# One step of a hybrid encoder layer on one core: where relu and square of the MLP's Strassen part run, and when mix's rows are stored

## The chip, the cores and the metric

The kernel runs on one core of one Trainium2 chip. The metric is the device time of one launch in microseconds (us). Three runs of the kernel before gave 2861.73, 2862.52 and 2863.64 us; the median is 2862.52 us.

The engines by the profile's names: PE is TensorE (matmuls) and PEld its weight loads, DVE is VectorE, ACT is ScalarE, POOL is GpSimd, SP is SyncE, which here only issues DMAs. PEq, ACTq and so on are the engines' instruction queues.

## The reference, cut to what matters

One layer works on 2048 prompt rows and 64 sample rows of width 1024, all in float32:

```python
h = rms_norm(x, g_pre_mix)
q, k, v, logf, gate_b, cu = project(h, w_in, b_f)
merged = concat(rms_norm(attention(q, k, v, logf)), rms_norm(gate_b * short_conv(cu)))
x = x + rms_norm(merged @ w_o, g_post_mix)          # "mix"
h2 = rms_norm(x, g_pre_mlp)
m = square(relu(h2 @ w_up)) @ w_down                # w_up 1024x4096, w_down 4096x1024
x = x + rms_norm(m, g_post_mlp)
```

Outputs are x for both row sets, the new keys, values, forget logs and the last rows of the convolution.

## The kernel before, in words

Float32 products are made of three matmuls on rounded operands: a value is split into a rounded high part (`hi`, type fp32r, usually written by ACT with a Copy) and the rest (`lo`, written by POOL or DVE as value minus hi), and hi*hi + hi*lo + lo*hi is summed in PSUM.

Three stages follow one another: input projection with attention, the output projection "mix" (`mix_rows`), and the MLP (`mlp`). All order is written out by hand: each engine has its own program, and semaphores join them (`wait_ge`, `then_inc`). An engine runs its program strictly in order, so an instruction that waits holds up all behind it on that engine.

**Mix.** The loop goes over 17 row tiles (tile 0 is the 64 sample rows) in software-pipelined steps t. In step t ACT squares the inputs of tile t+1 (L1782), rounds its convolution half (L1786), squares tile t-1's mixed rows (L1800), takes a root (L1804), squares the new x (L1808, with the store of x2, L1810), takes the next root (L1812), copies the attention part (`take_part`, L1819) and copies the transposed h2 of tile t-1 out of PSUM (`back_out`, L1827). `store_h2` issues the store of h2 to HBM on ACT's queue. For the first five tiles ("split", stored in hi and lo) it stands in front of `back_out` and stores tile t-2; for all later ones it stands behind `back_out` and stores tile t-1, the tile just copied (L1833). `h2_hi` has two slots, so `back_out` of tile t-1 waits until the store of tile t-3 has landed. PE transposes h2 (L2020) between the products of one tile and the next; it needs h2 from DVE (L1923), which stands at the end of the chain L1800, L1804, DVE's scaling and adding, L1808, L1812.

**MLP.** The rows are in three groups. Group 0 (5 tiles) is computed plainly. Groups 1 and 2 (6 row tiles each) make their first layer by Strassen's scheme: the hidden axis has 16 chunks of 256 columns, and for each chunk `up` makes 7 products of 12 matmuls (128x384) instead of 8. `down` then multiplies the 256 hidden values into 6 row tiles, 12 matmuls (128x512) each, in two alternating PSUM buffers. PE's order is up(chunk n+1), down(chunk n), up(n+2), and so on.

For a chunk, ACT copies the first product to SBUF (`take`, L2575); DVE's `combine` adds the other products (`plus`, L2683) into four results c11, c12, c21, c22 in the buffers `stage`, and applies relu and square to each in one instruction in place (`square`, L2669). Between them it makes four weight sums for the chunk after (`make_sum`, L2666), which the 7 products need. ACT's `hidden_first` waits until PE has done 3 (first half: c11, c12) or all 6 tiles (second half: c22, c21) of the previous `down`, since the hidden buffer is single, and copies them rounded (L2586); POOL's `hidden_rest` makes the lo part (L2454). After `combine` DVE adds each finished tile of `down` into y (`add`, L2728; L2726 in a group's first chunk). PE's third tile waits for the first add, the fourth for the second, and so on.

PE waits for DVE in three more places of `up`: products 5, 6 and 7 reuse PSUM buffers, and wait for `take`, the first `plus` and the c11 `plus`. The last stands behind the first weight sum, which waits for the DMA of the next raw weights.

At a group's end the finished rows are normalised: ACT squares and sums (`deviation`, L2597, and L2599), DVE scales (`scale`, L2771), POOL adds x (`out_rows`, L2462), SP stores (`store_y`). Four deviations stand on ACT between the two halves of `hidden_first`, and the remaining ones follow `take` of the next chunk. On SP the load of the raw weights of the chunk after next is queued behind the store of the group's second row tile, which waits for POOL's second `out_rows`. The late scales of a group stand in the next `combine` on DVE.

Of the kernel before, what the change touches and what calls it, by code (L numbers as in the profile page):

```python
# [7 lines left out]
ALU = mybir.AluOpType  # L8
ACT = mybir.ActivationFunctionType
# [20 lines left out]
RT = QT + 1  # L30
# [1618 lines left out]
def mix_rows(nc, io, dr, sem, ident, early, front, block, last_rows):  # L1649
# [8 lines left out]
    with ctx:  # L1658
# [25 lines left out]
        def at(t):  # L1684

            if isinstance(t, int) and t == 0:
                return SEQ, DEC
            return (t - 1) * P, P

        def run(eng, step):  # L1690

            for t in range(7):
                step(t, t % 2)
            with eng.Fori(0, 2) as i:
                step(2 * i + 7, 1)
                step(2 * i + 8, 0)
            for t in range(11, RT + 1):
                step(t, t % 2)

        def is_split(t):  # L1700

            return isinstance(t, int) and t < FIRST_TILES
# [7 lines left out]
        def is_tile(t):  # L1710
            return not isinstance(t, int) or 0 <= t < RT
# [65 lines left out]
        def _(act):  # L1777
# [51 lines left out]
            def store_h2(t, s):  # L1829
                row, n = at(t)  # L1830
                if not is_split(t):
                    act.wait_ge(S["h2_hi_done"], 2 * t + 2)
                    act.dma_start(dr["h2_t"].rearrange("(k p) r -> p k r", p=P)[:, :, bass.ds(row, n)], h2_hi[:, s, :, 0:n].bitcast(F32)).then_inc(h2_stored[s], 16)  # L1833
                    return
                act.wait_ge(S["h2_lo_done"], 2 * t + 2)
                for part, name in ((h2_hi, "h2_hi"), (h2_lo, "h2_lo")):
                    act.dma_start(dr[name].rearrange("(k p) r -> p k r", p=P)[:, :, bass.ds(row, n)], part[:, s, :, 0:n].bitcast(F32)).then_inc(h2_stored[s], 16)
# [5 lines left out]
            def step(t, s):  # L1843
                last, nxt = not isinstance(t, int) or t >= 1, is_tile(t + 1)
                if nxt:
                    front_squares(t + 1, 1 - s)
                final = isinstance(t, int) and t == RT
                if final:
                    act.wait_ge(S["c_mult"], RT)
                    early.split_first(act, 0)  # L1850
                if last:
                    back_squares(t - 1)
                    back_root(t - 1)
                if final:
                    early.split_first(act, 1)
                if nxt:
                    front_turned(t + 1, 1 - s)
                    if not last:
                        take_part(t, s)
                    front_root(t + 1, 1 - s)  # L1860
                if last:
                    back_second(t - 1, 1 - s)
                if is_tile(t) and last:
                    take_part(t, s)
                if is_split(t - 2) and t >= 2:
                    store_h2(t - 2, s)
                if last:
                    back_out(t - 1, 1 - s)
                    if not is_split(t - 1):
                        store_h2(t - 1, 1 - s)  # L1870

            run(act, step)

        @block.vector
        def _(dve):
# [223 lines left out]
def mlp(nc, io, dr, sem, early, front):  # L2099
# [13 lines left out]
    with ctx:  # L2113
# [19 lines left out]
        stage = [tile("m_stage0", [P, 3 * P])]  # L2133
# [45 lines left out]
        c11_taken, c12_taken, c21_taken, c22_taken = sem("m_c11_taken"), sem("m_c12_taken"), sem("m_c21_taken"), sem("m_c22_taken")  # L2179
        u_done = sem("m_u_done")  # L2180
# [12 lines left out]
        def chunk(g, i):  # L2193

            return CHUNKS * (g - 1) + i
# [56 lines left out]
        def is_first(g, i):  # L2252
            return isinstance(i, int) and i == 0
# [256 lines left out]
        def _(act):  # L2510
# [65 lines left out]

            def hidden_first(g, i, which):
                n, w = chunk(g, i), GROUP_COLS[g]
                if is_first(g, i):
                    act.wait_ge(dn_done, tiles_before(g, i) - (0 if which or g == 1 else COUNT[g - 1] - 3))  # L2580
                else:
                    act.wait_ge(dn_done, tiles_before(g, i - 1) + (COUNT[g] if which else 3))
                for r, b, src, seen in ((0, 0, 0, 1), (0, 1, 2, 3)) if which == 0 else ((1, 1, 3, 2), (1, 0, 1, 4)):
                    act.wait_ge(u_done, 4 * n + seen)
                    for x, hi, _ in hidden_parts(g, b, r, stage[src][:, 0:w]):
                        first = act.activation(hi, x, ACT.Copy)  # L2586
                    first.then_inc(u_hi_done, 1)
# [65 lines left out]
        def _(dve):  # L2653
# [11 lines left out]
                                (t1[:, :, :], b22, ALU.subtract, t2[:, :, :]), (t4[:, :, :], b21, ALU.subtract, t2[:, :, :]))[r]  # L2665
                dve.tensor_tensor(to, x, z, op).then_inc(sums_made, 1)  # L2666

            def square(x):
                return dve.scalar_tensor_tensor(x, x, 0.0, x, ALU.max, ALU.mult)  # L2669

            def combine(g, i, late=(), ahead=None):

                def sums(r):
                    if ahead:
                        make_sum(*ahead, r)

                n, w = chunk(g, i), GROUP_COLS[g]
                bank = [up_bank[b][:, 0:w] for b in BANK_OF]
                c11, c21, c12, c22 = (x[:, 0:w] for x in stage)

                def plus(j, to, x, done):
                    dve.wait_ge(multiplied, PRODUCTS * n + j + 1)
                    dve.tensor_tensor(to, bank[j], x, ALU.add).then_inc(done, 1)  # L2683

                later = not isinstance(n, int) or n >= 1
                dve.wait_ge(p1_taken, n + 1)
                if later:
                    dve.wait_ge(u_lo_done, 4 * n - 2)
                plus(1, c12, c11, p6_added)
                sums(0)  # L2690
                plus(2, c11, c11, c11_taken)
                dve.wait_ge(c11_taken, n + 1)
                square(c11).then_inc(u_done, 1)
                sums(1)
                dve.wait_ge(p6_added, n + 1)
                if later:
                    dve.wait_ge(u_lo_done, 4 * n)
                plus(3, c21, c12, p7_added)
                sums(2)
                dve.wait_ge(p7_added, n + 1)  # L2700
                plus(4, c22, c21, c22_taken)
                plus(4, c12, c12, p5_added)
                dve.wait_ge(c22_taken, n + 1)
                square(c22).then_inc(u_done, 1)
                sums(3)
                for f in late[:1]:
                    scale(f)
                dve.wait_ge(p5_added, n + 1)
                plus(5, c12, c12, c12_taken)
                dve.wait_ge(c12_taken, n + 1)  # L2710
                square(c12).then_inc(u_done, 1)
                plus(6, c21, c21, c21_taken)
                dve.wait_ge(c21_taken, n + 1)
                square(c21).then_inc(u_done, 1)
                for f in late[1:]:
                    scale(f)

# [281 lines left out]
```

## Time and profile before

| | |
|---|---|
| median of 3 runs | 2862.52 us |
| profiled execution, its own time | 2863.82 us |
| its span | 2862.2 us |
| PE busy | 2700.8 us, 94% |
| DVE busy | 1743.7 us, 61% |
| POOL busy | 1322.6 us, 46% |
| ACT busy | 998.1 us, 35% |
| mean granted TensorE clock | 0.987 of full speed |

A group of instructions is shown as line, engine, operation, output<-input, sizes, count, then busy time and mean time of one. The span counts from the first to the last instruction of the profiled execution; its own time is 1.6 us more. "Idle before" is the time an engine did nothing ahead of an instruction, with the instruction that released it. Times on a timeline are us from the span's start. Mix's loop lies at about 1107 to 1340, group 0 of the MLP at 1340 to 1804, group 1 from 1784, group 2 from about 2300.

### The profile page before, as it was taken

How to read it: one execution, taken by the hardware profiler on the slowest of the kernel's cores; microseconds unless marked ns; L12 is line 12 of the kernel's file. 1: busy time of each engine (PE TensorE's matmuls, PEld its weight loads, DVE VectorE, ACT ScalarE, POOL GpSimd, SP SyncE). 2: the span in 40 equal slices, each digit the busy share in tenths (PEclk: the TensorE clock that was granted, in tenths of full speed). 3: DMA queues.
4: the chain of work that ended last, by engine and by line, in shares of the span. 5: the costliest groups of instructions: out<-in, count | busy, mean ns of one | idle time of the engine just before them, and what ended most of it. 6: DMA issues, size and time to landing. Idle time of an engine off the chain costs nothing.

```text
span 2862.2 us, 42917 instructions
## 1 busy us (share of the span) xinstructions
PE 2700.8 (94%) x14966; PEld 2415.6 (84%) x14966; DVE 1743.7 (61%) x2744; ACT 998.1 (35%) x1831; POOL 1322.6 (46%) x883
## 2 busy tenths in 40 slices
PE   8999999999999999998999998899999989999997
PEld 8899899998787787877888887788888878888886
DVE  5333443348787886665445555777667756667775
ACT  3201201117787776544232322322222232222222
POOL 4233334311100126452567675765566657556664
PEclk9999999999999999999999999999999999999999
DMA  6534535665433443675344446422112352211213
GB/s 196 188 114 125 159 102 153 208 177 126 120 95 97 110 143 89 204 205 162 115 169 158 161 150 240 145 71 72 59 59 73 119 212 88 73 59 59 73 59 103
DMA packets 294358, 364.21 MB, mean 127 GB/s; under 512 B 37577, under 2 KB 245393, under 8 KB 290129
## 3 DMA queue, kind: packets, MB, share of 16 engines
q1 hardware_dynamic: 257152, 316.15, 36.1%
q0 software_dynamic: 11808, 26.74, 2.9%
q10 hardware_dynamic: 25264, 19.66, 2.0%
q8 instruction: 69, 1.13, 0.2%
q14 instruction: 65, 0.52, 0.1%
HBM read 264.30 MB, written 97.94 MB: 127 GB/s over the span
## 4 chain that ended last, share of the span: by engine, by line
PE 20%; DVE 13%; issue 10%; POOL 6%; DMA 2%; SPq 0%; ACT 0%; DVEq 0%; POOLq 0%; ACTq 0%
PE dn_bank L2902 13%; PE up_bank L2877 6%; DVE m_t L2666 4%; DVE m_raw_up L2666 3%; DVE m_stage L2683 3%; POOL m_pieces L2438 2%; POOL m_up_plain L2415 2%; DMA m_raw_up<-in_w_up 2%; POOL m_u L2431 2%; DVE m_y L2728 1%; PE up_bank L2833 1%; PE dn_bank L2857 1%; DMA m_raw_dn<-in_w_down 1%; DVE m_y L2771 1%; DVE m_stage L2669 1%
## 5 line engine op out<-in xcount | busy, mean ns | idle before, releaser
L2902 PE MATMUL dn_bank<-m_w_dn,m_u 128*128 128x512 f32 x2304 | 543.0, 394 | 39.6 <-DVE m_y L2728 29.2
L2902 PEld LDWEIGHTS dn_bank<-m_w_dn,m_u 128*128 128x128 f32 x2304 | 434.0, 190 | 140.9 <-DVE m_y L2728 38.7
L2877 PE MATMUL up_bank<-m_h,m_w_up 128*128 128x384 f32 x2688 | 476.3, 337 | 10.3 <-DVE m_stage L2683 6.5
L2877 PEld LDWEIGHTS up_bank<-m_h,m_w_up 128*128 128x128 f32 x2688 | 470.8, 189 | 14.0 <-issue 11.4
L2728 DVE TENSOR_TENSOR m_y<-dn_bank,m_y 128x1024 f32<-128x1024 f32 x180 | 217.6, 1220 | 194.4 <-PE dn_bank L2902 194.1
L508 POOL TENSOR_TENSOR w_lo<-w_raw,w_hi 128x1024 fp32r<-128x1024 f32 x72 | 181.0, 2518 | 327.8 <-DVE w_hi L722 327.8
L2454 POOL TENSOR_TENSOR m_u<-m_stage,m_u 128x384 fp32r<-128x384 f32 x128 | 130.5, 1040 | 280.7 <-ACT m_u L2586 280.7
L2411 POOL TENSOR_TENSOR m_w_up<-m_raw_up,m_w_up 128x512 fp32r<-128x512 f32 x128 | 196.2, 1552 | 83.0 <-ACT m_w_up L2560 83.0
L2743 DVE TENSOR_TENSOR m_u<-m_u 128x320 f32<-128x320 f32 (+1 forms) x64 | 109.3, 1747 | 174.9 <-ACT m_u L2540 174.9
L2586 ACT ACTIVATE m_u<-m_stage 128x384 fp32r<-128x384 f32 x128 | 60.1, 517 | 438.6 <-PE dn_bank L2902 437.5
L938 PE MATMUL proj<-ha_hi,w_hi 128*128 128x384 f32 (+1 forms) x640 | 212.2, 332 | 0.0
L1452 DVE TENSOR_TENSOR p_lo<-t_bank,p_hi 128x512 fp32r<-128x512 f32 (+1 forms) x336 | 198.4, 600 | 20.3 <-ACT p_hi L1393 18.0
L2833 PEld LDWEIGHTS up_bank<-m_h,m_up_plain 128*128 128x128 f32 x1536 | 206.4, 189 | 4.6 <-issue 2.0
L938 PE MATMUL proj<-ha_hi,w_lo 128*128 128x384 f32 (+1 forms) x640 | 210.1, 328 | 0.0
L938 PE MATMUL proj<-ha_lo,w_hi 128*128 128x384 f32 (+1 forms) x640 | 210.0, 328 | 0.0
L2833 PE MATMUL up_bank<-m_h,m_up_plain 128*128 128x256 f32 (+1 forms) x1536 | 208.0, 295 | 1.7 <-PEq L2966 1.7
L1349 POOL TENSOR_TENSOR att<-o_n 128x256 f32<-128x256 f32 (+1 forms) x40 | 26.2, 656 | 392.2 <-ACT o_n L1404 387.9
L1393 ACT ACTIVATE p_hi<-t_bank 128x512 fp32r<-128x512 f32 (+1 forms) x336 | 171.8, 528 | 71.3 <-PE t_bank L1490 67.2
L2683 DVE TENSOR_TENSOR m_stage<-up_bank,m_stage 128x384 f32<-128x384 f32 x224 | 119.9, 546 | 93.9 <-PE up_bank L2877 93.9
L2560 ACT ACTIVATE m_w_up<-m_raw_up 128x512 fp32r<-128x512 f32 x128 | 76.4, 625 | 251.0 <-PE up_bank L2877 221.6
L2447 POOL TENSOR_TENSOR m_w_dn<-m_raw_dn,m_w_dn 128x2048 fp32r<-128x2048 f32 x32 | 147.8, 4620 | 20.4 <-ACT m_w_dn L2568 20.2
L2411 POOL TENSOR_TENSOR m_w_up<-m_t,m_w_up 128x512 fp32r<-128x512 f32 x96 | 151.7, 1607 | 0.0
(290 smaller groups left out, 5809.5 us busy)
## 6 DMA issues: line engine op xcount, KB each, us to landing
m_raw_up<-in_w_up SPq DMA_DIRECT2D x48, 1024.0 KB, 5.4
m_raw_dn<-in_w_down SPq DMA_DIRECT2D x48, 1024.0 KB, 4.9
w_raw<-in_w_in SPq DMA_DIRECT2D x72, 512.0 KB, 4.1
scratch_h_pairs<-m_pieces POOLq DMA_DIRECT2D x12, 1792.0 KB, 7.8
m_h<-scratch_h_pairs SPq DMA_DIRECT2D x14, 1536.0 KB, 11.2
nck<-scratch_ncum SPq DMA_DIRECT2D x8, 1312.0 KB, 18.6
scratch_v_hl<-vhl SPq DMA_DIRECT2D x20, 512.0 KB, 2.7
q_hi<-scratch_q_hi SPq DMA_DIRECT2D x16, 528.0 KB, 6.9
```

The source lines that it names most:

```text
L508: pool.tensor_tensor(w_lo[:, slot(i)], w_raw[:, i % 2], w_hi[:, slot(i)].bitcast(F32), ALU.subtract).then_inc(w_lo_done, 1)
L938: mm = pe.matmul(out[:, 0:CW[g]], w[:, slot(i), k], h[g][:, k, chunk(g, n)], start=(k == 0 and a == 0), stop=(k == KB - 1 and a == 2))
L1393: act.activation(p_hi[:, x.p, x.cols], t_bank[x.at % T_BANKS][:, x.cols], ACT.Copy).then_inc(hi_done, 1)
L1452: dve.tensor_tensor(p_lo[:, x.p, x.cols], t_bank[x.at % T_BANKS][:, x.cols], p_hi[:, x.p, x.cols].bitcast(F32), ALU.subtract).then_inc(lo_ ...
L2411: pool.tensor_tensor(w_up[:, j, 1], sources[j], w_up[:, j, 0].bitcast(F32), ALU.subtract).then_inc(w_lo_done, 1)
L2447: pool.tensor_tensor(w[:, 1], raw[:, :, :], w[:, 0].bitcast(F32), ALU.subtract).then_inc(dn_lo_done, 1)
L2666: dve.tensor_tensor(to, x, z, op).then_inc(sums_made, 1)
L2683: dve.tensor_tensor(to, bank[j], x, ALU.add).then_inc(done, 1)
L2728: dve.tensor_tensor(place, bank[:, :], place, ALU.add).then_inc(y_added, 1)
L2833: mm = pe.matmul(up_bank[2 * x + b][:, 0:w], up_first[:, cc, wp, k, b * P:(b + 1) * P], early.rows[2 * x + hp][:, k, :], start=(k == 0 and ...
L2877: mm = pe.matmul(out, w_up[:, j, wp, k, :], hidden_rows(g, j, hp, k), start=(k == 0 and p == 0), stop=(k == KH - 1 and p == 2))
L2902: mm = pe.matmul(bank[:, cols], part, wd[:, wp, b, cols], start=(b == 0 and p == 0), stop=(b == 1 and p == len(passes) - 1))
```

## The change

The MLP: DVE's `square` and its waits go. ACT's `hidden_first` gets, for each of the two results of its half, a wait for the result, a Relu in place and a Square in place (the Square waits for the Relu), and then one wait for both, all ahead of the wait for PE's tiles. The rounding copies stay as they are. Mix: the store of h2 is ahead of `back_out` for every tile, and stores tile t-2; the last tile's store follows the loop.

```diff
             def step(t, s):
...
-                if is_split(t - 2) and t >= 2:
+                if not isinstance(t, int) or t >= 2:
                     store_h2(t - 2, s)
                 if last:
                     back_out(t - 1, 1 - s)
-                    if not is_split(t - 1):
-                        store_h2(t - 1, 1 - s)
 
             run(act, step)
+            store_h2(RT - 1, (RT - 1) % 2)
...
             def hidden_first(g, i, which):
                 n, w = chunk(g, i), GROUP_COLS[g]
+                for m, (src, taken) in enumerate(((0, c11_taken), (2, c12_taken)) if which == 0 else ((3, c22_taken), (1, c21_taken))):
+                    x = stage[src][:, 0:w]
+                    act.wait_ge(taken, n + 1)
+                    act.activation(x, x, ACT.Relu).then_inc(u_done, 1)
+                    act.wait_ge(u_done, 8 * n + 4 * which + 2 * m + 1)
+                    act.activation(x, x, ACT.Square).then_inc(u_done, 1)
+                act.wait_ge(u_done, 8 * n + 4 * which + 4)
                 if is_first(g, i):
                     act.wait_ge(dn_done, ...)
                 else:
                     act.wait_ge(dn_done, ...)
-                for r, b, src, seen in ((0, 0, 0, 1), (0, 1, 2, 3)) if which == 0 else ((1, 1, 3, 2), (1, 0, 1, 4)):
-                    act.wait_ge(u_done, 4 * n + seen)
+                for r, b, src in ((0, 0, 0), (0, 1, 2)) if which == 0 else ((1, 1, 3), (1, 0, 1)):
                     for x, hi, _ in hidden_parts(g, b, r, stage[src][:, 0:w]):
                         first = act.activation(hi, x, ACT.Copy)
...
-            def square(x):
-                return dve.scalar_tensor_tensor(x, x, 0.0, x, ALU.max, ALU.mult)
...
                 plus(2, c11, c11, c11_taken)
-                dve.wait_ge(c11_taken, n + 1)
-                square(c11).then_inc(u_done, 1)
                 sums(1)
...
                 plus(4, c12, c12, p5_added)
-                dve.wait_ge(c22_taken, n + 1)
-                square(c22).then_inc(u_done, 1)
                 sums(3)
...
                 plus(5, c12, c12, c12_taken)
-                dve.wait_ge(c12_taken, n + 1)
-                square(c12).then_inc(u_done, 1)
                 plus(6, c21, c21, c21_taken)
-                dve.wait_ge(c21_taken, n + 1)
-                square(c21).then_inc(u_done, 1)
```

## Rows read from the trace of the kernel before

**Rows 1.** The page, part 1: busy time, share of the span and instructions.

```profile
PE 2700.8 (94%) x14966; PEld 2415.6 (84%) x14966; DVE 1743.7 (61%) x2744; ACT 998.1 (35%) x1831; POOL 1322.6 (46%) x883
```

**Rows 2.** Timeline of PE in the Strassen groups: start, length, instructions, idle before.

```profile
1902.43 11.18 PE L2902 MATMUL dn_bank<-m_w_dn,m_u 128*128 128x512 f32 x48 [0.93 <-DVE m_y L2728]
...
1998.96 11.17 PE L2902 MATMUL dn_bank<-m_w_dn,m_u 128*128 128x512 f32 x48 [0.94 <-DVE m_y L2728]
2009.98 14.74 PE L2877 MATMUL up_bank<-m_h,m_w_up 128*128 128x384 f32 x84
...
2788.16 11.20 PE L2902 MATMUL dn_bank<-m_w_dn,m_u 128*128 128x512 f32 x48 [0.94 <-DVE m_y L2728]
```

**Rows 3.** Timeline of DVE, a middle chunk's end and the last chunk's last product.

```profile
2028.30 0.54 DVE L2683 TENSOR_TENSOR m_stage<-up_bank,m_stage 128x384 f32<-128x384 f32 x1
2029.87 1.21 DVE L2728 TENSOR_TENSOR m_y<-dn_bank,m_y 128x1024 f32<-128x1024 f32 x1
...
2813.97 0.56 DVE L2683 TENSOR_TENSOR m_stage<-up_bank,m_stage 128x384 f32<-128x384 f32 x1 [0.86 <-PE up_bank L2877]
```

**Rows 4.** DVE's squares, all 128: duration in ns, minimum, median, maximum.

```profile
L2669 DVE SCALAR_TENSOR_TENSOR m_stage<-m_stage x128: 540/1069/2386, 1794.2 to 2814.6; 128x384 f32<-128x384 f32 x128
```

**Rows 5.** Timeline of ACT in the same middle chunk.

```profile
2002.09 0.94 ACT L2586 ACTIVATE m_u<-m_stage 128x384 fp32r<-128x384 f32 x2 [6.72 <-PE dn_bank L2902]
2010.25 0.94 ACT L2586 ACTIVATE m_u<-m_stage 128x384 fp32r<-128x384 f32 x2 [7.22 <-PE dn_bank L2902]
```

**Rows 6.** Timelines of PE, ACT, POOL and DVE where group 1 begins.

```profile
1816.12 6.82 PE L2877 MATMUL up_bank<-m_h,m_w_up 128*128 128x384 f32 x24 [3.81 <-ACT m_stage L2575]
1827.25 3.38 PE L2877 MATMUL up_bank<-m_h,m_w_up 128*128 128x384 f32 x12 [4.31 <-DVE m_stage L2683]
...
1839.29 11.18 PE L2902 MATMUL dn_bank<-m_w_dn,m_u 128*128 128x512 f32 x48 [2.70 <-DVE m_y L2726]
...
1807.39 1.06 ACT L2597 ACTIVATE m_junk<-m_y 64x1024 bf16<-64x1024 f32 x1 [2.45 <-DVE m_y L2763]
...
1814.00 2.35 POOL L2462 TENSOR_TENSOR m_y<-m_y,m_x 128x1024 f32<-128x1024 f32 x1 [1.16 <-DVE m_y L2771]
...
1824.06 2.58 DVE L2666 TENSOR_TENSOR m_raw_up<-m_raw_up 128x512 f32<-128x512 f32 x1 [6.17 <-DMA m_raw_up<-in_w_up]
```

**Rows 7.** The same where group 2 begins: PE, DVE and POOL.

```profile
2312.61 2.34 PE L2877 MATMUL up_bank<-m_h,m_w_up 128*128 128x384 f32 x12 [0.38 <-DVE m_stage L2683]
...
2324.65 13.66 PE L2902 MATMUL dn_bank<-m_w_dn,m_u 128*128 128x512 f32 x48 [4.25 <-DVE m_y L2728]
...
2352.60 2.31 PE L2877 MATMUL up_bank<-m_h,m_w_up 128*128 128x384 f32 x12 [1.78 <-DVE m_stage L2683]
...
2368.13 14.07 PE L2902 MATMUL dn_bank<-m_w_dn,m_u 128*128 128x512 f32 x48 [7.74 <-DVE m_y L2726]
...
2311.30 0.69 DVE L2666 TENSOR_TENSOR m_raw_up<-m_raw_up 128x512 f32<-128x512 f32 x1 [6.70 <-DMA m_raw_up<-in_w_up]
...
2323.39 2.34 DVE L2728 TENSOR_TENSOR m_y<-dn_bank,m_y 128x1024 f32<-128x1024 f32 x2
...
2358.61 2.38 DVE L2669 SCALAR_TENSOR_TENSOR m_stage<-m_stage 128x384 f32<-128x384 f32 x1
...
2358.18 2.39 POOL L2462 TENSOR_TENSOR m_y<-m_y,m_x 128x1024 f32<-128x1024 f32 x1 [6.75 <-DVE m_y L2771]
```

**Rows 8.** Mix: timelines of ACT and PE; landing of the x2 stores (L1810).

```profile
1236.35 1.09 ACT L1827 ACTIVATE h_hi<-h_bank 128x512 f32<-128x512 f32 x2 [1.34 <-PE h_bank L2020]
1237.60 0.38 ACTq L1833 DMA_DIRECT2D scratch_h_t<-h_hi  x1
1238.08 0.63 ACT L1782 ACTIVATE junk_a<-a_in 128x512 f32<-128x512 f32 x1 [0.64 <-ACT h_hi L1827]
...
1209.22 1.09 PE L2020 MATMUL h_bank<-ident,h 128*128 128x128 f32 x8 [1.25 <-DVE h L1923]
...
1288.93 1.10 PE L2020 MATMUL h_bank<-ident,h 128*128 128x128 f32 x8 [0.96 <-DVE h L1923]
...
DMA to landing us min/median/max: 2.6/5.5/11.7
```

## The prediction, made before the run

> **What bounds the kernel now.** I read the page's busy times first: PE is busy for 94% of the span, no other engine for more than 61% [rows 1]. So PE sets the time, and a change that leaves the matmuls alone can only give back PE's idle time or slow spells. There are about 160 us outside PE's busy time; the question is how many of these the change touches. The second view was the timeline of PE, of which I kept the rows with idle time before them. In the Strassen groups the same row comes back every 32.18 us: 48 matmuls of `down` (the third to sixth tile) start after 0.94 us of idle, released by DVE's add [rows 2]. I count 25 such rows: 13 in group 1 (first 1902.43, last 2288.55) and 12 in group 2 (2434.16 to 2788.16). Around them lie the larger stalls at the two group changes [rows 6, 7], and in mix seven short ones before the transposes [rows 8]. Third, the timelines of DVE, ACT and POOL for what ended each of these.
>
> **Steady chunks.** Take the chunk whose `up` starts at 2009.98. `up` takes 14.74 us for 84 matmuls, less a small overlap: `down` follows 14.58 later. Had DVE been free, the last `plus` could have started when the seventh product came, 14.77 us after the start: in the last chunk, where DVE makes no weight sums, that is 2813.97 against 2799.20 for PE [rows 3]. In the middle chunk it starts at 2028.30, so 18.32, and the first add at 2029.87, so 19.89; yet the first tile of `down` is done about 17.5 us after the start (14.58 plus one sixth of the 16.8 us that six tiles take). DVE is late by 2.35 us there; PE, having a second buffer, loses 0.94 of it.
>
> The change takes four squares of mostly 1.07 us from DVE ahead of this add, starts overlapping by some 0.08: 4.0 us. A square can take as little as 0.54 [rows 4], and the difference might be waiting for POOL that passes to the next instruction; then only 4 x 0.54 = 2.16 us go. Both exceed 0.94, and with DVE no earlier than the seventh product (14.77 + 0.56 = 15.3) it then waits for the first tile. The whole 0.94 goes, the period becomes 31.24 us. What is late next: nothing on DVE; PE has its next `up` buffers freed by `plus` instructions that all come earlier.
>
> On ACT each chunk gains 8 instructions. None of this shape is there with Relu, but a rounding copy from the same buffer is: two in 0.94 us [rows 5]. Lower bound 0.47 each, upper bound, with the wait of Square for Relu, 0.60; I take 0.55, so 2.2 us per half. What hides it: ACT sits idle for 6.72 us before the first half's copies and 7.22 us before the second half's [rows 5], each time for PE's tiles. Queued behind the new waits on ACT are the copies, `take` and the weight copies. c12's `plus` ends about 15.3 us after the start, just as ACT is through with its last weight copy (2027.5, or 17.5, before, and pulled forward by the earlier sums), so the four instructions end near 18 and the copies are due at 22. POOL's lo parts and PE's wait for them do not move. If the cover were gone, each us would fall on the copies, then on `take`, which product 5 needs only 8.4 us into `up`: still some 5 us of slack. Cost on the path: nothing.
>
> The stall at 2288.55 I leave to the group change below: 24 x 0.94 = **22.6 us**.
>
> **First group change [rows 6].** PE loses 3.81 + 4.31 + 2.70 = 10.8 us. (a) The 3.81 is `take` on ACT, which stands behind four deviations and the second half's copies. The deviations wait 2.45 us for DVE's fold, which follows `combine` and comes about 3.8 us sooner without squares; so they start 2.45 sooner, and four new instructions of 2.2 us follow them: 0.25 us is won, nearly nothing. (b) The 4.31 is product 7, which waits for DVE's first weight sum, that for the DMA landing at 1824.06, its issue for POOL's second `out_rows` (1814.00 to 1816.35), that for the second deviation and scale. All of these are ahead of the four new instructions, so the DMA lands 2.5 to 2.9 us sooner; I take 2.8. (c) From landing to the first copies into y at 1838.02 DVE needs 13.96 us, of which squares are .56, .55, 2.39 and .56, less overlap 3.8. The 2.39 is not arithmetic. The same pattern stands in rows 7: the square starts at 2358.61 while POOL runs from 2358.18 to 2360.57, and ends 0.42 after POOL does. The next such DVE instruction would then wait for POOL: with the square gone that is the scale behind the last `plus`, 1.1 us after POOL starts, which would lose about 1 us. I take 2.9. Sum 2.8 + 2.9 = **5.7 us**; bounds 0 (the new ACT work eats it) and 8.
>
> The Trainium skill, SBUF — State Buffer, section "SBUF: two separate sides", says the port pair that VectorE shares with GpSimd is locked for a whole instruction, and a VectorE instruction with two SBUF inputs is blocked until the GpSimd one ends. By that rule a removed square gives back its arithmetic and hands its wait on, as I took it in (c); by the rows' durations alone (c) would be 3.8 and the total 0.9 us more here. The trace agrees with the rule where the square ends 0.42 us after POOL [rows 7].
>
> **Second group change [rows 7].** Product 7 at 2312.61 waits for a DMA (landed 2311.30) whose queue is full of row loads that began with the chunk before; it stays where it is, and eats the 0.94 us of the stall at 2288.55. Then DVE takes from 2311.30 to 2323.39 to reach its first add; four squares of this stretch (1.21, 0.71, 1.04, 1.03, less overlap) go: **3.7 us**, of a stall of 4.25. In that stretch PE then has no stall above 1.3 us. Today the 48 matmuls after the 4.25 us take 13.66 us instead of 11.17: the granted clock fell to its lower level (1.2 GHz, against 2.4) after the idle time. After stalls of 0.94 and 1.78 us rows show full speed (11.17 for 48; 2.31 for 12) [rows 2, 7]; so the **2.5 us** come back too. The next `up` shifts along; its product 7 (stall 1.78) depends on the adds, scales and `out_rows` after that, and is 0.4 us less late. Last, the 7.74 us before 2368.13: as (c) above, four squares .56, .55, 2.38, .56, but two or more scales follow and take over POOL's wait: 2.7 us, leaving about 5 us of stall, and with it the slow 14.07. Sum 3.7 + 2.5 + 0.4 + 2.7 = **9.3 us**; bounds 3.7 and 13.
>
> The end of the kernel (last `down`, scales) has neither squares nor stores of this kind: 0.
>
> **Mix.** Today the next square on ACT (1238.08) starts 0.64 us after `back_out` ended (1237.44), with the store of 0.38 between them; elsewhere ACT starts such an instruction about 0.1 us before the one ahead ends. So the store costs about 0.7 us, at the head of the chain that makes h2, for which PE waits before the transposes. Now it is issued where ACT waits 1.34 us for PE anyway [rows 8]: hidden. The seven stalls of PE are 1.25, 0.26, 0.73, 0.23, 0.67, 0.47 and 0.96, together 4.57, of which the first and the last are shown [rows 8]; 0.7 less of each (1.25 less at the first, whose store took longer) leaves under 0.5: about 4.1. But part of the later ones is a loop branch, so I take 3.8. At the last tile the same store stands ahead of a chain that is all path: 0.6. Sum **4.4 us**, bounds 2 and 5.2. The added wait: `back_out` now needs a store issued one tile (13 us) earlier instead of two; the stores of x2, of the same size and queue, landed in 2.6 to 11.7 us [rows 8]. Nothing waits.
>
> **Sum.** 22.6 + 5.7 + 9.3 + 4.4 = 42.0 us. The profiled execution would go from 2863.82 to 2821.8; it lies 1.3 above the median of the runs, so I expect a median of 2862.5 - 42.0 = 2820.5, rounded to **2821 us**. Lower bounds together: 22.6 + 0 + 3.7 + 2 = 28.3, so 2834; upper ones 22.6 + 8 + 13 + 5.2 = 48.8, so 2814.
>
> **Rivals.**
> (A) The group changes give nothing: ACT's new work behind the deviations delays `take` by its whole 2.2 us, PE's clock falls as before, DVE waits for POOL instead of squaring. For it: ACT is the releaser of the 3.81. Against: 2.45 us of idle just ahead, and loads that hang on the early deviations. Then 22.6 + 4.4 = 27 us, 2835.5.
> (B) No change to be measured: DVE's squares are mostly waiting for POOL, the wait passes to the next weight sum, and the add stays late. It needs less than 0.94 us saved per chunk, less than two bare squares. Then only mix's 4.4 us: 2858.
> (C) Slower: the h2 stores land too late for `back_out`. Two stores now go out within some 4 us of each other on ACT's queue, and at 1260 to 1300 the DMA engines are also busy with early loads for the MLP. `back_out` of ten tiles waits for a store issued about 13.1 us before. Each us beyond that delays ACT, then PE, by a us in each of ten tiles; to outweigh 42 us it takes 4.2 us each, a landing after 17.3 us. The x2 stores' maximum is 11.7, so this needs half as much again. At a landing of 18.5 us: 54 - 42, so 2874.
>
> **How the numbers follow.** Forecast 0.85, A 0.08, B 0.04, C 0.03. 0.2%, about what this kernel's measurement can tell from no change, is 5.7 us. Forecast and A are faster: 0.93. B is the same: 0.04; C slower: 0.03. The range is that of the bounds, 2814 to 2834; A, B and C lie outside and hold 0.15.
>
> **What would show it.** Right: PE's rows of 48 matmuls follow without idle, 31.2 us apart; DVE idle ahead of the first add; ACT's idle before its copies down to about 4.5 to 5; no slow spell after the first `down` of group 2's start, but still one after the next. In mix no idle above 0.5 us before PE's transposes, and the last one 0.6 shorter. Wrong: the 0.94 stays, or returns with ACT or POOL as its releaser; `take` later in relation to product 5; idle before `back_out` released by a DMA.

## The result, and the profile after

The changed kernel takes 2812.64 us (median of 4 runs, 2811.65 to 2812.99); the kernel before, run beside it, 2863.08 (2861.73 to 2864.92). The ratio is 0.9823 with an interval of 0.9806 to 0.9840. I had predicted 2821 us and a range of 2814 to 2834: the sign and the mechanism were right, the gain was 50.4 us instead of 42.0, and the time lies 1.4 us below the range. The profiled execution took 2812.99 us, 50.8 less than the one before, so the two traces can be compared row by row.

Part 1 of the page after answers to [rows 1]. VectorE (DVE) lost 128 instructions, ScalarE (ACT) gained 256, and TensorE (PE) is busy for 96% of a shorter span:

```profile
PE 2689.5 (96%) x14966; PEld 2417.6 (86%) x14966; DVE 1574.0 (56%) x2616; ACT 1113.7 (40%) x2087; POOL 1283.6 (46%) x883
```

PE has the same 14966 matmuls as before and yet 11.3 us less busy time. That is the first sign of what I had missed.

The timeline of PE in the Strassen groups (columns: start, length, instructions) answers to [rows 2]. The 72 matmuls of `down` stand in one row, with no idle time in them, and one `up` starts 30.94 us after the other:

```profile
1963.18 14.74 PE L2871 MATMUL up_bank<-m_h,m_w_up 128*128 128x384 f32 x84
1977.77 16.52 PE L2896 MATMUL dn_bank<-m_w_dn,m_u 128*128 128x512 f32 x72
1994.12 14.74 PE L2871 MATMUL up_bank<-m_h,m_w_up 128*128 128x384 f32 x84
```

The timeline of DVE in that chunk answers to [rows 3]: it now waits for PE before the last `plus` and again before the first add (idle time in brackets):

```profile
1976.22 0.54 DVE L2685 TENSOR_TENSOR m_stage<-up_bank,m_stage 128x384 f32<-128x384 f32 x1
1977.96 0.56 DVE L2685 TENSOR_TENSOR m_stage<-up_bank,m_stage 128x384 f32<-128x384 f32 x1 [1.20 <-PE up_bank L2871]
1980.72 1.23 DVE L2722 TENSOR_TENSOR m_y<-dn_bank,m_y 128x1024 f32<-128x1024 f32 x1 [2.20 <-PE dn_bank L2896]
```

ACT, answering to [rows 5]. The four new instructions of the first half go from 1978.51 to 1980.55, 2.04 us, and 5.6 and 5.3 us of idle time are left before the copies:

```profile
1978.51 0.51 ACT L2581 ACTIVATE m_stage<-m_stage 128x384 f32<-128x384 f32 x1
1979.05 0.53 ACT L2583 ACTIVATE m_stage<-m_stage 128x384 f32<-128x384 f32 x1
...
1986.16 0.94 ACT L2591 ACTIVATE m_u<-m_stage 128x384 fp32r<-128x384 f32 x2 [5.62 <-PE dn_bank L2896]
...
1994.32 0.94 ACT L2591 ACTIVATE m_u<-m_stage 128x384 fp32r<-128x384 f32 x2 [5.28 <-PE dn_bank L2896]
```

PE at the two group changes, answering to [rows 6, 7]. Where there were 3.81, 4.31 and 2.70 us of idle time there are 3.39, 1.93 and none; where there were 0.38, 4.25, 1.78 and 7.74 there are 1.64, none, 1.77 and 3.36, and one slow row of 48 matmuls instead of two. But the two rows behind the 1.77 us are slow now (12 matmuls in 3.02 us and 24 in 6.54, mean granted clock 0.82 of full speed), where the same rows before took 2.31 and 5.64 at a granted clock of 1.00:

```profile
1810.11 7.17 PE L2871 MATMUL up_bank<-m_h,m_w_up 128*128 128x384 f32 x24 [3.39 <-ACT m_stage L2574]
1819.20 3.88 PE L2871 MATMUL up_bank<-m_h,m_w_up 128*128 128x384 f32 x12 [1.93 <-DVE m_stage L2685]
1822.92 16.66 PE L2896 MATMUL dn_bank<-m_w_dn,m_u 128*128 128x512 f32 x72
1839.42 14.74 PE L2871 MATMUL up_bank<-m_h,m_w_up 128*128 128x384 f32 x84
...
2286.89 2.33 PE L2871 MATMUL up_bank<-m_h,m_w_up 128*128 128x384 f32 x12 [1.64 <-DVE m_stage L2685]
2289.06 16.52 PE L2896 MATMUL dn_bank<-m_w_dn,m_u 128*128 128x512 f32 x72
...
2319.86 3.02 PE L2871 MATMUL up_bank<-m_h,m_w_up 128*128 128x384 f32 x12 [1.77 <-DVE m_stage L2685]
...
2332.58 13.88 PE L2896 MATMUL dn_bank<-m_w_dn,m_u 128*128 128x512 f32 x48 [3.36 <-DVE m_y L2720]
2346.29 14.74 PE L2871 MATMUL up_bank<-m_h,m_w_up 128*128 128x384 f32 x84
```

Mix, answering to [rows 8]. On ACT the store is issued while `back_out` still waits for PE, and the next square starts before the copies end; PE's transposes have no idle time before them but at the last tile:

```profile
1216.32 0.38 ACTq L1833 DMA_DIRECT2D scratch_h_t<-h_hi  x1
1218.99 1.09 ACT L1827 ACTIVATE h_hi<-h_bank 128x512 f32<-128x512 f32 x2 [1.71 <-PE h_bank L2019]
1219.97 0.63 ACT L1782 ACTIVATE junk_a<-a_in 128x512 f32<-128x512 f32 x1
...
1208.14 1.04 PE L2019 MATMUL h_bank<-ident,h 128*128 128x128 f32 x8
1220.63 1.04 PE L2019 MATMUL h_bank<-ident,h 128*128 128x128 f32 x8
...
1327.81 1.97 PE L2019 MATMUL h_bank<-ident,h 128*128 128x128 f32 x8 [9.10 <-DVE h L1922]
```

**Where the time came from.** I cut both timelines of PE at the same instructions, by their starts:

| stretch | before | after | difference | predicted |
|---|---|---|---|---|
| start to mix's first tile | 1107.54 | 1105.53 | -2.0 | 0 |
| mix, to the first matmul of the MLP | 232.80 | 225.91 | -6.9 | -4.4 |
| group 0 (without Strassen) | 443.38 | 446.35 | +3.0 | 0 |
| start of group 1 | 66.59 | 61.63 | -5.0 | -5.7 |
| group 1, steady, to product 7 of group 2's first chunk | 462.30 | 447.47 | -14.8 | -11.3 |
| start of group 2 | 69.43 | 59.40 | -10.0 | -9.3 |
| group 2, steady, to its last wait | 449.67 | 434.73 | -14.9 | -11.3 |
| end | 30.49 | 30.28 | -0.2 | 0 |

The sum is -50.9. The first and third lines are unchanged code and cancel to 1 us; in the profiled executions of the ten kernels below the first cut lies between 1105.2 and 1107.9 and group 0 takes 441.6 to 445.2, so I take these two for scatter. The 446.35 lies 1.2 above that range; there the trace after has one wait for POOL of 2.80 us with 32 matmuls in 10.35 us behind it, which the trace before doesn't have. What is left to explain is the steady chunks (29.8 for 22.6) and mix (6.9 for 4.4).

**The missing third of a microsecond.** Before, two `up` rows around a stalled `down` are 32.18 us apart; the period after is 30.94. The stall shown in the row is 0.94, the difference 1.24. Before's own trace has a chunk without the stall, and it too is short: windows of both (columns: start:end and length, then busy time and count of PE, PE's weight loads, DVE, ACT, POOL, granted clock, DMA share, GB/s):

```profile
1850.31:1881.28 30.97, 30.97 (x158) 28.02 (x156) 21.53 (x21) 8.15 (x13) 20.52 (x13) 1.00 0.32 102
1977.80:2009.98 32.18, 31.24 (x158) 28.02 (x156) 22.65 (x21) 8.04 (x13) 19.57 (x12) 1.00 0.21 65
```

The same window after:

```profile
1963.18:1994.12 30.94, 30.94 (x157) 28.10 (x156) 17.11 (x17) 11.68 (x21) 18.32 (x12) 1.00 0.21 68
```

The same 156 matmuls are busy for 31.24 us with one wait among them and for 30.97 or 30.94 with none. So a wait of 0.94 us costs PE another 0.3 us that the view books as busy. It stood in the trace that I predicted from.

### The profile page after: what moved, and what is told of

Its sections match the earlier page's. It is cut to its first block, busy times and chain, and to the rows that moved or that the text cites. A ratio compares the mean times of both kernels' runs of the same rounds, so it can differ in the third digit from the quotient of the medians.

```text
span 2811.3 us, 43099 instructions
## 1 busy us (share of the span) xinstructions
PE 2689.5 (96%) x14966; PEld 2417.6 (86%) x14966; DVE 1574.0 (56%) x2616; ACT 1113.7 (40%) x2087; POOL 1283.6 (46%) x883
## 3 DMA queue, kind: packets, MB, share of 16 engines
q8 instruction: 69, 1.13, 0.2%
## 4 chain that ended last, share of the span: by engine, by line
PE 36%; POOL 6%; issue 6%; DVE 2%; DMA 2%; SPq 0%; ACT 0%; POOLq 0%; ACTq 0%; DVEq 0%
PE dn_bank L2896 18%; PE up_bank L2871 15%; POOL m_pieces L2437 2%; POOL m_up_plain L2414 2%; PE dn_bank L2851 1%; POOL m_u L2430 1%; DMA m_raw_up<-in_w_up 1%; PE up_bank L2827 1%; DMA m_raw_dn<-in_w_down 1%; DVE m_y L2765 1%; DVE m_u L2737 0%; SPq L2289 0%; POOL m_w_dn_even L2419 0%; DVE m_y L2722 0%; DVE m_raw_up L2671 0%
## 5 line engine op out<-in xcount | busy, mean ns | idle before, releaser
L2896 PE MATMUL dn_bank<-m_w_dn,m_u 128*128 128x512 f32 x2304 | 532.8, 392 | 4.8 <-DVE m_y L2720 3.4
L2410 POOL TENSOR_TENSOR m_w_up<-m_raw_up,m_w_up 128x512 fp32r<-128x512 f32 x128 | 190.3, 1507 | 83.6 <-ACT m_w_up L2559 83.6
L1506 PE MATMUL o_bank<-p_hi,v_hl 128*128 128x512 f32 (+3 forms) x360 | 140.5, 398 | 9.2 <-DVE p_lo L1452 9.2
```

The lines of the kernel that those rows point to most:

```text
L1506: pe.matmul(out, v_hl[par][:, vb, :], p_hi[:, t.p, at], start=x.first and i == 0, stop=False)
L2410: pool.tensor_tensor(w_up[:, j, 1], sources[j], w_up[:, j, 0].bitcast(F32), ALU.subtract).then_inc(w_lo_done, 1)
L2896: mm = pe.matmul(bank[:, cols], part, wd[:, wp, b, cols], start=(b == 0 and p == 0), stop=(b == 1 and p == len(passes) - 1))
```

## The experiments

Theory A: the change removes waits of PE as forecast, and each wait costs 0.3 us more than its row shows. Theory B is its rival: the forecast's terms are right, and the other 8 us come from somewhere else (the chance of one execution, mix, the group changes, the clock, or fewer instructions on DVE in itself).

**One part at a time.** `e1_mlp_only` is the changed kernel with the store where it was:

```
-                if not isinstance(t, int) or t >= 2:
+                if is_split(t - 2) and t >= 2:
                     store_h2(t - 2, s)
...
                     back_out(t - 1, 1 - s)
+                    if not is_split(t - 1):
+                        store_h2(t - 1, 1 - s)
```

> The MLP's half of the change alone; mix stores as before. Theory A: the changed kernel gained 50.4 us, 8 more than forecast, because each wait of PE costs more than the idle time its row shows: in the kernel before, chunks without the stall are 30.97 us apart and those with it 32.17, so 1.2 and not 0.94 (25 times), and the same holds for mix's seven stalls. Then this run gains about 43 to 44 us: 2819 to 2820. Theory B: the extra 8 us are chance of the execution (the part of the kernel ahead of mix, which is unchanged, is 2.0 us shorter in the changed kernel's trace): then 2824 to 2828. The period of a middle chunk: 30.94 in theory A, and no 48-matmul row with idle ahead.

`e2_store_only` is the kernel before with the store moved and the squares left on DVE.

> Mix's store one tile later, alone; the MLP as before. Theory A (each of PE's seven waits costs its shown idle of 4.57 us in sum plus some 0.25 us each, and the last chain 0.6): a gain of 6.9 us, 2856.2. Theory B (the shown idle is the whole cost, as forecast): 4.4 us, 2858.7. A rival to both: the store's place matters nothing and the mix part of the trace is shorter by chance: 2863.

Measured: 2819.91 us for the first, ratio 0.9851 (0.9837 to 0.9864), so -42.0 us; 2854.48 for the second, 0.9971 (0.9959 to 0.9982), so -7.4. The first time lies in what A expects (2819 to 2820) and not in what B does (2824 to 2828). The second gain has an interval of 5.2 to 11.7 us, which holds A's 6.9 and leaves B's 4.4 just outside. Together they make 49.4 of the 50.4 us: within the intervals the parts add up and don't help each other. In the trace of the second mix takes 225.83 us instead of 232.80, and the stall in the chunks stands as before (timeline of PE):

```profile
1994.74 11.22 PE L2901 MATMUL dn_bank<-m_w_dn,m_u 128*128 128x512 f32 x48 [0.93 <-DVE m_y L2727]
```

Mix shows the same hidden term. These are three transposes of the kernel before (timeline of PE); after, the tiles are 12.49 us apart:

```profile
1222.20 1.09 PE L2020 MATMUL h_bank<-ident,h 128*128 128x128 f32 x8 [0.26 <-DVE h L1923]
...
1235.67 1.09 PE L2020 MATMUL h_bank<-ident,h 128*128 128x128 f32 x8 [0.73 <-DVE h L1923]
...
1248.64 1.09 PE L2020 MATMUL h_bank<-ident,h 128*128 128x128 f32 x8 [0.23 <-DVE h L1923]
```

13.47 less 12.49 is 0.98 for 0.73 shown, and 12.97 less 12.49 is 0.48 for 0.23 shown: 0.25 more in both. Seven waits make 4.57 + 7 x 0.25 = 6.3, and with 0.62 at the last tile (9.72 to 9.10) the 6.9 us of the table.

**A wait without any square.** In the changed kernel DVE was filled with reductions that nobody reads, 1.13 us each, before the adds of 26 chunks: three of them (no more than its idle time and PE's second buffer cover), four (a wait of about the old size), five (about a microsecond more):

```
                 plus(6, c21, c21, c21_taken)
+                if not isinstance(i, int):
+                    for r in range(4):
+                        dve.tensor_reduce(fill[:, r:r + 1], g_post[:, :], AX.X, ALU.max)
```

> The changed kernel with four reductions of 1024 numbers on DVE (their results unused) between the last product's addition and the adds into y, in 26 of the 32 chunks. DVE has 2.25 us of idle there and PE's second buffer covers 1.27 more, 3.5 in sum; four reductions at about 1.1 us are 4.5, so the stall comes back with about 1.0 us of real loss per chunk, without any square on DVE. Theory A: the period grows from 30.94 by 0.25 to 0.3 us more than the idle that PE's rows show (say 31.9 with 0.7 shown), in all 26 us slower than the changed kernel, 2839. Theory B (the 0.3 came with the squares, not with the wait): the period grows by just the idle shown.

> As the run with four reductions (period 32.07 with 0.81 us of idle shown, against 30.94 and none), with five. The fifth takes 1.13 us, all of it past the cover. Theory A (each wait of PE costs a fixed 0.3 us beyond the idle shown, as its matmuls end 0.39 us after they start but follow one another every 0.23): the period grows by 1.13 to 33.2, the idle shown by the same 1.13 to 1.94, the difference stays 0.3; in all 29 us slower, 2869. Rival: the excess is a share of the idle (0.3 of 0.8), then it grows to 0.7 and the period to 33.6, 2879.

> As the runs with four and five reductions on DVE ahead of the adds (real loss 1.13 and 2.24 us per stalled chunk at full clock), with three. The cover is 4 x 1.13 - 0.81 - ... that is, the first add must be through about 3.5 us after the last product's addition plus its own time; three take 3.4. Both theories of the cost of a wait expect no idle and a period of 30.94 to 31.0, 2812.6 in all: the filling itself costs nothing, and DVE is not in the way of PE while it works. If the period grew by some 0.3 without any idle shown, the cost would not be the wait's.

Each of the three ran once. Three reductions: 2814.09 us, a period of 30.97, no idle time. Filled time on DVE costs nothing by itself, which speaks against B's last form. Four: 2839.74. Timeline of PE, and the filling on DVE:

```profile
1965.90 14.74 PE L2875 MATMUL up_bank<-m_h,m_w_up 128*128 128x384 f32 x84
1980.48 5.64 PE L2900 MATMUL dn_bank<-m_w_dn,m_u 128*128 128x512 f32 x24
1986.93 11.22 PE L2900 MATMUL dn_bank<-m_w_dn,m_u 128*128 128x512 f32 x48 [0.81 <-DVE m_y L2726]
1997.98 1.23 PE L2875 MATMUL up_bank<-m_h,m_w_up 128*128 128x384 f32 x6
...
1981.15 4.59 DVE L2712 TENSOR_REDUCE m_fill<-m_g_post 128x1 f32<-128x1024 f32 x4
```

The period is 32.08 us, 1.14 over 30.94, and the row shows 0.81: 0.33 is hidden, in a kernel with no square on DVE. Five gave 2893.87, which neither theory had. The trace shows why:

```profile
1939.13 14.74 PE L2875 MATMUL up_bank<-m_h,m_w_up 128*128 128x384 f32 x84
...
1961.29 11.18 PE L2900 MATMUL dn_bank<-m_w_dn,m_u 128*128 128x512 f32 x48 [1.93 <-DVE m_y L2726]
1972.31 14.74 PE L2875 MATMUL up_bank<-m_h,m_w_up 128*128 128x384 f32 x84
...
1994.46 12.78 PE L2900 MATMUL dn_bank<-m_w_dn,m_u 128*128 128x512 f32 x48 [1.93 <-DVE m_y L2726]
2007.08 3.13 PE L2875 MATMUL up_bank<-m_h,m_w_up 128*128 128x384 f32 x17
```

The first chunk shown takes 33.18 us, 2.24 over 30.94 with 1.93 shown, as A has it. In the next the 48 matmuls after the same wait take 12.78 us instead of 11.18, part of them at 1.2 GHz instead of 2.4 (mean granted clock 0.86 in this row, 1.00 in the one before), and the period is 34.77. So a wait of 1.93 us can cost twice what its row shows. Of the 26 such rows 15 are slow (12.76 to 12.80) and 11 at full speed (11.17 to 11.19), in no order that I could explain; 26 x 2.24 + 15 x 1.6 is 82 us, and the kernel is 81 slower. The hidden 0.3 us held; the clock was a cost that I had left out of both theories.

**How much had to leave DVE.** `e7_half` gives c22's and c21's squares back to DVE, and ACT keeps those of c11 and c12:

```
...
                 plus(4, c12, c12, p5_added)
+                dve.wait_ge(c22_taken, n + 1)
+                square(c22).then_inc(second_done, 1)
...
                 plus(6, c21, c21, c21_taken)
+                dve.wait_ge(c21_taken, n + 1)
+                square(c21).then_inc(second_done, 1)
```

> Half of the MLP change: ACT squares c11 and c12, DVE keeps the fused relu and square of c22 and c21, as before the change. The forecast's claim: a steady chunk needs only 1.2 us less on DVE, and two of four squares give that; so the period is 30.94 and no idle stands before the third tile. At group 1's beginning ACT is freed of 2.1 us ahead of its copy of the first product (stall 3.39): 0 to 2 us gained there; at group 2's DVE is later by about 1.5: lost again. 2811 to 2814. Rival: two squares do not suffice since the wait for POOL passes on; then the period is 31.2 or more and the time 2820 or more.

2814.19 us, 0.9829 (0.9812 to 0.9845), the same as the whole change within the intervals; the period of a steady chunk is 30.94 (1962.33 to 1993.27) with no stall. Two squares suffice there; the prediction had put the need at less than two bare squares. At the group changes its stalls are others (in the first 1.32 instead of 3.39 at product 5 and 6.82 instead of 1.93 at product 7, in the second 6.10 instead of 3.36 before the third tile), and nothing is won.

**What is left at the group changes.** Two edits on the changed kernel, alone and together. `e4_early_load` loads the raw weights of a group's third chunk, on whose landing product 7's wait hangs, ahead of the row loads and of the stores of y; `e5_late` puts the last scales of a group between the next group's first adds:

```
+                load_up(2, CHUNKS + 2 * PRODUCTS)
                 load_x(1)
...
-                if ahead:
+                if ahead and not is_first(g, i):
                     load_up(ahead[1], CHUNKS + PRODUCTS * chunk(*ahead))
...
                     if g < 2:
+                        load_up(2, CHUNKS + PRODUCTS * (chunk(g + 1, 2)))
                         store_y(f)
```

```
                 plus(6, c21, c21, c21_taken)
-                for f in late[1:]:
-                    scale(f)
...
+                rest = [f for f in range(FIRST_ITEM[g - 1] + 4, FIRST_ITEM[g])] if is_first(g, i) else []
                 for k in range(COUNT[g]):
                     add(g, i, k)
+                    for f in rest[k:k + 1]:
+                        scale(f)
```

> The changed kernel, with the load of the raw weights for the third chunk of groups 1 and 2 ahead of the stores of the previous group's first two row tiles on SP's queue, instead of behind them. Theory A: these loads land late only because they queue behind the stores, and PE's stalls before product 7 (1.93 and 1.77 us), before the third tile in group 2's first down (3.36) and the slow clock after them (about 0.7 and 2.9) hang on the landing: 7 to 11 us faster than the changed kernel, about 2804. Rival: the DMA engines are full there with row loads and the landing does not move, or the wait returns with the late scales on DVE: within 3 us of 2812.6.

> The changed kernel with a finished group's last scales (one in group 1's first down, two in group 2's) moved on DVE from ahead of the first adds to between them. Theory: PE's 3.36 us before the third tile at group 2's beginning, and the slow clock after it (48 matmuls in 13.88 instead of 11.02 us), hang on these two scales (2.5 and 3.4 us, most of it waiting for POOL): about 6 us faster than the changed kernel, 2806 to 2807; at group 1's beginning nothing, as no idle is shown there. Rival: the wait for POOL returns at the next instruction, or POOL's rows and the stores behind them come too late for the adds of tiles 5 and 6: within 2 us of 2812.6.

> Both moves together: the early weight loads and the late scales. With the early loads alone the stalls before product 7 went, but 3.77 us (group 1) and 5.70 us (group 2) came before the third tile, as a weight sum on DVE now waits 4.6 us for one POOL instruction. Theory: these two stalls end with the scales out of the way (2.5, and 2.5 + 3.4 us of DVE time), with the slow clock after them: 2799 to 2803. Rival: DVE stays late through the weight sums that wait for POOL, 1.3 us of stall at least in group 1: 2805 or more.

Each alone missed what its theory expected: 2810.81 us, 0.9817 (0.9802 to 0.9832), and 2810.27, 0.9812 (0.9793 to 0.9830). Both intervals overlap that of the change itself. The rivals that let the wait return elsewhere came nearer, and the traces show the waits move. With early weights product 7 no longer waits, but the third tile of `down` does (PE; then DVE and POOL at the same time):

```profile
2330.04 13.50 PE L2898 MATMUL dn_bank<-m_w_dn,m_u 128*128 128x512 f32 x48 [5.70 <-DVE m_y L2722]
...
2311.05 5.00 DVE L2673 TENSOR_TENSOR m_t<-m_raw_up 128x512 f32<-128x512 f32 x1
...
2310.89 4.62 POOL L2448 TENSOR_TENSOR m_w_dn<-m_raw_dn,m_w_dn 128x2048 fp32r<-128x2048 f32 x1
```

With late scales the `down` that had been stalled runs whole, but in the next chunk product 7 waits 4.96 us for the c11 `plus`. That stands behind a weight sum, which DVE starts at the landing of the raw weights and which takes 7.03 us beside POOL's instructions (timelines of PE and DVE):

```profile
2320.43 16.52 PE L2897 MATMUL dn_bank<-m_w_dn,m_u 128*128 128x512 f32 x72
2336.79 12.70 PE L2872 MATMUL up_bank<-m_h,m_w_up 128*128 128x384 f32 x72
2354.45 3.65 PE L2872 MATMUL up_bank<-m_h,m_w_up 128*128 128x384 f32 x12 [4.96 <-DVE m_stage L2685]
...
2346.81 7.03 DVE L2671 TENSOR_TENSOR m_raw_up<-m_raw_up 128x512 f32<-128x512 f32 x1 [3.01 <-DMA m_raw_up<-in_w_up]
```

Together, `e6_late_early` takes 2800.91 us (2799.81 to 2803.14), ratio 0.9783 (0.9766 to 0.9799): as expected, 11.7 us less than the change, and the best version. At the second group change, what was 1.77 and 3.36 with a slow row of 13.88 is now one of 0.32, and one of 1.37 at product 7 of the next chunk. At the first, product 5 still waits 3.39, and the 1.93 at product 7 has become 0.83 before the third tile and 1.07 at the next product 7. PE's timeline of the second:

```profile
2315.93 11.08 PE L2899 MATMUL dn_bank<-m_w_dn,m_u 128*128 128x512 f32 x48
2327.33 5.78 PE L2899 MATMUL dn_bank<-m_w_dn,m_u 128*128 128x512 f32 x24 [0.32 <-DVE m_y L2720]
...
2347.09 2.33 PE L2874 MATMUL up_bank<-m_h,m_w_up 128*128 128x384 f32 x12 [1.37 <-DVE m_stage L2687]
```

`e8_first` adds to it what `e7_half` had shown at product 5: in the first Strassen chunk alone, c22's and c21's squares on DVE.

> Early weight loads and late scales (2800.9) and, in the first chunk of group 1 alone, relu and square of c22 and c21 back on DVE, so that ACT has 2.1 us less ahead of its copy of the first product. With all chunks so, PE's stall before product 5 went from 3.39 to 1.32, but the weights came late; here they come early. Theory: 2 to 4 us less, 2797 to 2799. Rival: DVE, which then is 1.1 to 1.6 us later, gives it back before the third tile (stall 0.83 there now): 2801 to 2803.

2801.33 us, 0.9787 (0.9770 to 0.9803): the theory missed. The rival's time came out, but not by its wait before the third tile: the wait at product 5 fell from 3.39 to 1.31, and a new one of 3.06, released by POOL, came before `down`, with 72 matmuls in 18.23 instead of 16.5 us:

```profile
1805.76 6.48 PE L2886 MATMUL up_bank<-m_h,m_w_up 128*128 128x384 f32 x36 [1.31 <-ACT m_stage L2577]
1815.31 18.23 PE L2911 MATMUL dn_bank<-m_w_dn,m_u 128*128 128x512 f32 x72 [3.06 <-POOL m_w_dn L2449]
```

## Why the prediction was right in kind and too small in size

**Steady chunks: the term that failed.** The step is "The whole 0.94 goes, the period becomes 31.24 us". The whole wait went, but the period became 30.94, in all 25 chunks: 1.24 instead of 0.94 each. The table has 29.8 us for the steady stretches. That is 25 x 1.24 = 31.0 less the 1.27 us that product 7 took back (0.38 to 1.64, below); the forecast had 22.6. I took the idle time in a row for PE's loss. But the row's idle time begins at the modelled end of the last matmul, and matmuls overlap: single rows of 128x512 last 0.39 us and start 0.23 after one another. Of a matmul that is followed at once, 0.16 us of the 0.39 are covered by the next; at a wait they lie bare and are booked as busy. The restart is slower too: the first matmul after the wait lasts 0.50 us and the next starts 0.34 later instead of 0.23 (PE before):

```profile
1998.96 0.50 PE L2902 MATMUL dn_bank<-m_w_dn,m_u 128*128 128x512 f32 x1 [0.94 <-DVE m_y L2728]
...
1999.30 0.62 PE L2902 MATMUL dn_bank<-m_w_dn,m_u 128*128 128x512 f32 x2
```

0.94 + 0.16 + 0.11 is 1.21, the difference of 32.18 and 30.97 in the trace before; the last 0.03 lies between the two traces. The two parts are read from rows with modelled ends, so how the 0.30 divides is argued; that it is 0.3 is shown by the periods at 0.94 (1.24), 0.81 (1.14) and 1.93 (2.24).

The Trainium skill, TensorE: Matmul & The Clock Gate, section "Single matmul latency", gives (398 + N) / 2.4 ns for a single bf16 matmul of N columns at the full clock; that is an estimate of 379 ns at N = 512. The trace's 0.39 us is near it, but its ends are modelled and its operands are not bf16, so this is no check. The Trainium skill, Perfetto Trace Analysis, section "Identifying the Most-Contended Engine", says that matmul busy time is no good measure of how near the engine is to its limit, because pipelined instructions look smaller in the trace. The windows above agree that it is no good measure, with 31.24 and 30.97 us busy for equal work.

The rest of this step held. (19.89 less 17.5 is 2.39, not the 2.35 that stands there; no term used it.) DVE waits for PE's seventh product and for the first tile. ACT's new instructions took 0.51 to 0.53 us, 2.04 a half (I had 0.55 and 2.2), and cost the path nothing; ACT's idle time is 5.6 and 5.3 instead of 4.5 to 5. `e7_half` shows that two squares less would do in these chunks.

**First group change: 5.0 for 5.7.** The 3.81 fell by 0.42 (I had said nearly nothing, 0.25). What was short is the landing of the raw weights: 2.1 us sooner, not the 2.8 of (b). It hangs on the deviations, and these had only 2.45 us of idle time to give, as (a) itself says. Now they follow the rounding copies at once, and those wait for PE (timeline of ACT after):

```profile
1798.47 0.94 ACT L2591 ACTIVATE m_u<-m_stage 128x384 fp32r<-128x384 f32 x2 [2.90 <-PE dn_bank L2851]
1799.31 1.04 ACT L2602 ACTIVATE m_junk<-m_y 64x1024 bf16<-64x1024 f32 x1
```

PE came 0.3 us later itself, as its `up` row ahead took 15.11 us for 14.78 (granted clock 0.98 after, 1.00 before). From the landing to DVE's first copies it is 11.15 us after for 13.96, 2.8 less where I had 2.9: the reading that the removed square hands its wait to the next scale held. The wait of 2.70 us behind it is gone whole, so more than that and its hidden 0.3 could not have been won there.

**Second group change: 10.0 for 9.3.** The sum is near, but partly by luck. Product 7 of the first chunk waits for its DMA as before, and eats 1.27 us of the stall that went ahead of it. The 4.25 went whole, with its hidden 0.3 and the 2.5 of the slow row: 7.0 where I had 3.7 + 2.5. The 0.4 for the 1.78 did not come (1.77). From the landing to the copies it is 14.70 us for 17.44, the 2.7 forecast, and from product 7's start to the third tile's it is 12.72 for 15.53, 2.8. That the wait before the third tile fell by 4.4 (7.74 to 3.36, where I had "about 5" left) is no further gain: the two rows behind the 1.77 us took 9.56 us instead of 7.95, as the clock was lower, and PE reached the wait 1.6 us later. I had counted the two as at full speed.

The Trainium skill, SBUF — State Buffer, section "SBUF: two separate sides", was the rule by which I took 2.9 and 2.7 instead of 3.8. The trace agrees once more in `e4_early_load`: a weight sum of DVE with both inputs in SBUF takes 5.00 us beside a POOL instruction of 4.62, from within 0.2 us of its start to 0.5 after its end, while the same sum takes 0.68 us alone.

**Mix: 6.9 for 4.4.** All seven waits went, and with them 0.25 us each that the rows hide. I also held back 0.8 us for loop branches and leftovers, of which nothing was seen: no transpose but the last has idle time before it. The last tile gave 0.62, as predicted (0.6).

**The rivals.** A is out: the group changes gave 15 us. B is out: the add is early and DVE idle. C is out: no instruction of ACT in mix waits for a DMA after; how near the landing came was not tested. The landing times in [rows 8] I had misread: 2.6/5.5/11.7 also counts the later loads of these rows in the MLP. The stores of x2 alone landed in 2.6 to 7.2 us before and 2.7 to 8.0 after, so C was less likely than I had made it. `e2_store_only` shows that the move gains by itself.

## What to carry to other kernels

Read what a wait costs PE from the distance between two like matmul rows, with and without the wait, not from the idle time shown in front of the row; the difference was 0.3 us, a third of a wait of 0.94, and 0.25 us at one of 0.23. From an engine that hands its work on late, only as much need go as it is late: here two of four squares gave all that the steady chunks had. At a stage change the idle time of a row can shrink because PE comes later, so measure from one like row to the next there too. And clear the wait and its neighbour on the other queue together: either edit alone mostly moved the wait (1.8 and 2.4 us, within the noise of the change), both together took 11.7 us.

## What the runs showed of the hardware

A wait of 1.93 us in each chunk of 33 us was enough for the granted clock to fall behind it in 15 of 26 chunks (48 matmuls in 12.78 us instead of 11.18). Waits of 0.81 to 0.94 us in as many chunks did nothing of the kind (11.17 to 11.22); after 3.36 and 5.70 us the rows take 13.88 and 13.50. Near 1.8 us it goes either way in the same place: behind a wait of 1.78 us before, 12 and 24 matmuls took 2.31 and 5.64 us, behind one of 1.77 after, 3.02 and 6.54. A wait of the tensor engine in this kernel is thus priced in two steps: 0.3 us over what is shown (0.25 before the transposes of mix), and some 1.6 us more for many of about 2 us.

A VectorE instruction with two inputs in SBUF can take as long as the GpSimd instruction beside it: a weight sum of 0.68 us took 5.00 beside one of 4.62.
